# A gated linear-attention stage placed between projections, and per-pair norm and rotation behind the next projection, in a two-block transformer kernel on one Trainium2 core

## The chip, the core and the metric

The kernel runs on one core of one Trainium2 chip. The core has a matrix engine (TensorE, PE in the profile, with its weight loads as PEld), a vector engine (VectorE, DVE), a scalar engine (ScalarE, ACT), GpSimd (POOL), and SyncE (SP), which here issues the weight transfers. The time is the device time of one execution in microseconds (us). Each engine works through its own instruction list in order; semaphores tie the lists together.

## What is computed

Two blocks of two layers each over 256 tokens of width 1024, all in 32-bit floats. Four mixers (differential attention, sparse attention, "even" and "odd") alternate with four expert stages. The change touches the even and the odd mixer, so only these are shown, cut.

```python
def even_mixer(x, w_in, ...):
    h = x @ w_in
    c_q, c_kv, k_pe, gq, gk, gv, g_lr, gr = _split(h, EVEN_SPLITS)   # 256,128,32,256,256,512,32,512
    q  = (rms_norm(c_q, mla_q_norm) @ w_uq)      # 8 heads, 64 plain + 32 rotated
    kv = (rms_norm(c_kv, mla_kv_norm) @ w_ukv)   # 8 heads, keys 64, values 64
    o_mla = mla_attention(...)                   # softmax attention over 256 tokens
    la_f = log_sigmoid(lr_f @ gate_w_fwd + gate_b_fwd) / 16     # la_b likewise
    o_f = gla_chunked(qh, kh, vh, la_f)          # 4 heads, key 64, value 128, 4 chunks of 64
    o_b = flip(gla_chunked(flip(qh), flip(kh), flip(vh), flip(la_b)))
    o_gla = rms_norm(o_f + o_b, gla_norm) * silu(gr)
    return concatenate([o_mla, o_gla])           # then @ w_o, residual, layer norm

def gla_chunked(q, k, v, log_a):
    cum = cumsum(log_a)                          # within a chunk
    qg, kg = q * exp(cum), k * exp(-cum)
    att = where(tri, qg @ kg.T, 0)
    u = (k * exp(last - cum)).T @ v              # the chunk's update of the state
    o = att @ v + qg @ state_before_the_chunk    # state = decay * state + u, chunk by chunk

def odd_mixer(x, w_in, ...):
    q, k, v = _split(x @ w_in, ODD_SPLITS)       # 1024, 256, 256
    q, k = rms_norm per head of 64, then apply_rope
    # grouped attention, 16 query and 4 key heads
```

## The kernel before, in words

The program is one hand-ordered list for each engine; nothing schedules it. Activations lie transposed in SBUF (`xT`, `hT`, `qT`, `kT`, `oT`, `yT`: 128 partitions by 8 pieces by 256 tokens). Weights flow through a ring of 12 slots of 1 MB each (`ring`): SP issues the transfer of slot n as soon as slot n-12 has been used (`slot_used`), in the order in which the jobs were declared. A **job** is one slice of a projection, at most 256 columns of a weight: `project(js)` on PE runs its matmuls into PSUM bank 0 or 1 in turn (16 matmuls of 128 by 128 by 256 for a full slice, L869), and `evacuate(js)` on ACT copies each bank out (L282). PE may start job j when job j-2 is evacuated.

**Even mixer.** PE runs the ten jobs of `w_in` (the slices for the compressed query and key, the shared key, gq, gk, two of gv, the gate's low rank, two of gr), then `partition_norms(1)`, the rms norms of the two compressed vectors, then the jobs of `w_uq` and `w_ukv` with rotations between them, then `attention("mla")`, then `gla_stage()`, then `partition_norms(2)` (rms norm of the gated output times silu), and only then the output projection `even_out`.

`gla_stage` is a chain over three engines: PE computes the gate's logits (L1310, L1312, 8 matmuls), ACT and DVE turn them into log decays (L1692 to L1697, L2167), PE sums them per chunk (L1320), ACT and DVE form qg, kg and kd (L1700 to L1704, L2174 to L2183), PE computes scores (L1331) and four transposes for each direction, DVE masks and copies (L2187, L2189), PE computes updates (L1344), DVE runs the state recurrence (L2200, L2202), PE computes the outputs (L1356 and L1362: 16 matmuls of 128 columns and 24 of 64), and DVE copies them out (L2210).

A norm along partitions (`pns`) takes: squares on ACT (L1556); `pn_sums` on PE (L908), matmuls with the squares as weights and one or two columns of ones; a root on ACT (L1564); a reciprocal on DVE (L1866); `pn_spread` on PE (L922), which spreads the factors over the partitions; and one product per vector on DVE (L1873). A rotation is one matmul on PE (L881) and three DVE instructions (L1857 to L1859).

**Odd mixer.** PE runs four query jobs, two key jobs and one value job, then all sums, then spread and rotation for six pairs of head pieces one after another; the attention begins when DVE has finished the last rotation (L2378, L1012).

The two output projections are followed by a layer norm, the router, and an expert stage whose weights (4 groups of 48 slots, `ring<-in_w`) come through the same ring.

Of the kernel before, what the change touches and what calls it, by code (L numbers as in the profile page):

```python
# [16 lines left out]
P = 128  # L17
T = 256
# [110 lines left out]
def program(nc, A, out):  # L129

    ctx = ExitStack()
    with ctx:
# [251 lines left out]
        for _ in ADA_STEP["nsa"]:  # L384
# [20 lines left out]
        job(ew[:, 0:256], 8, 256, mm_T(xT, 8, [(0, P, 0, 0), (P, P, 0, T)]),  # L405
            copy_to((whole, scr[:, 0:512])), need=("h_ready", 5))
        job(ew[:, 256:384], 8, 128, mm_T(xT, 8, [(0, P, 0, 0)]),
            copy_to((lambda b: ps[:, b, 0:T], ckvT[:, 0, :])))
        job(ew[:, 384:416], 8, 32, mm_T(xT, 8, [(0, 32, 64, 0)]),
            copy_to((lambda b: ps[64:96, b, 0:T], kpe[64:96, :])))  # L410
        ev_kpe = len(jobs) - 1
        job(ew[:, 416:672], 8, 256, mm_T(xT, 8, [(0, P, 0, 0), (P, P, 0, T)]), copy_to((whole, scr[:, 1024:1536])))
        job(ew[:, 672:928], 8, 256, mm_T(xT, 8, [(0, P, 0, 0), (P, P, 0, T)]), copy_to((whole, scr[:, 1536:2048])))
        for s in range(2):
            job(ew[:, 928 + 256 * s:1184 + 256 * s], 8, 256, mm_V(xT, 8, 256),
                copy_to((lambda b: ps[:, b, :].rearrange("p (a n) -> p a n", a=TT), gv[:, :, 256 * s:256 * s + 256])))
        job(ew[:, 1440:1472], 8, 32, mm_T(xT, 8, [(0, 16, 0, 0), (16, 16, 0, T)]),
            copy_to((lambda b: ps[0:16, b, :], rt[0:16, 0:512])))
        ev_lr = len(jobs) - 1
        for s in range(2):  # L420
            job(ew[:, 1472 + 256 * s:1728 + 256 * s], 8, 256, mm_T(xT, 8, [(0, P, 0, 0), (P, P, 0, T)]),
                copy_to((whole, hfl[:, 1024 + 512 * s:1536 + 512 * s]), func=ACT.Silu))
# [63 lines left out]
        dense(ow, xT, qT, 4, ("h_ready", 7))  # L486
        for s in range(2):
            job(ow[:, D + 128 * s:D + 128 * s + 128], 8, 128, mm_T(xT, 8, [(0, P, 0, 0)]),
                copy_to(*twice(kT[:, 2 * s:2 * s + 2, :])))
        job(ow[:, D + 256:D + 512], 8, 256, mm_V(xT, 8, 256), copy_to((whole, vt[:, 0:512])))  # L490
        vo = vt[:, 0:512].rearrange("p (a n) -> p a n", a=TT)
        ph["odd_out"] = len(jobs)
# [53 lines left out]
        r_odd = len(ropes)  # L546
        for s in range(6):
            ropes.append((pair_dst(qT if s < 4 else kT, s % 4), 2, 0, P, K("rot64"), K("cos_g"), K("sin_g"),
                          ("pn_done", 8 + s + 1)))
# [5 lines left out]
        for s in range(4):  # L555
# [4 lines left out]
                    ("job", ph["even"])))  # L560
        pns.append(([ckvT[:, 0, :]], K("ones")[:, 0:1], 128, [(ckvT[:, 0, :], col("mla_kv_norm_2"), ckvT[:, 0, :], None)],
                    ("job", ph["even"] + 1)))
# [4 lines left out]
        for s in range(6):  # L567
            o = pair_dst(qT if s < 4 else kT, s % 4)
            pns.append(([o], K("ones64")[:, 0:P:64], 64, [(o, col("gqa_q_norm_2" if s < 4 else "gqa_k_norm_2"), o, None)],
                        ("job", ph["odd"] + s)))  # L570

        pn_batch = [range(0, 4), range(4, 6), range(6, 8), range(8, 14)]

        def pn_columns(i, c, tt):

            batch = next(b for b in pn_batch if i in b)
            at = 0
            for x in range(batch[0], i):
                at += pns[x][0][0].shape[-1] // T * TT * pns[x][1].shape[-1]
# [3 lines left out]
        def pn_width(batch):  # L583
            last = batch[-1]
            return pn_columns(last, pns[last][0][0].shape[-1] // T - 1, TT - 1).stop
# [58 lines left out]
        soft["mla"] = [vt[:, 1024:2048], flat(oT)[:, 1024:2048]]  # L644
# [21 lines left out]
        kdt = [sg[:, 512 * d:512 * d + 512].rearrange("p (a n) -> p a n", a=TT) for d in range(2)]  # L666
# [1752 lines left out]
```

## Time and profile before

| | us |
|---|---|
| median of 3 runs | 2433.51 |
| lowest, highest | 2432.26, 2434.05 |
| the profiled execution's own time | 2425.88 |
| its span in the profile | 2424.1 |
| PE busy | 1852.0 (76%) |
| DVE busy, ACT busy | 429.3, 400.1 |
| mean granted TensorE clock | 0.878 of full speed |

The even mixer up to its output projection lies between 1007.3 and 1181.9 us of the span; the odd mixer's projections, norms and rotations between 1742.9 and 1820.0. In the rows below, PE is the matmul engine; the chain of waits gives a start, a duration and what ran; a count (x) counts instruction records, and a 32-bit matmul leaves two of them. "PEclk" is the share of full TensorE speed granted, 0.50 being 1.2 GHz and 1.00 being 2.4 GHz.

### The profile page before, as it was taken

The page shows a single profiled execution, that of the slowest core. Times are in us where ns is not written, and L with a number is a line of the kernel's source. Part 1 is how long each engine was busy: PE and PEld are TensorE (multiplying, and loading weights), DVE is VectorE, ACT ScalarE, POOL GpSimd, SP SyncE. Part 2 cuts the span into 40 slices and gives each one's busy share as a digit, 9 for nine tenths or more (in the row PEclk, how much of TensorE's full clock was granted, in tenths as well). Part 3 has the DMA queues.
Part 4 walks back from the last instruction along what each step waited for, and adds up shares of the span by engine and source line. Part 5 has one row for each costly group of instructions (what it writes and reads, how often), then busy time and mean ns, then how long its engine had stood idle before and what let it go on. Part 6 is the DMA issues. An engine that isn't in the chain of part 4 may idle for free.

```text
span 2424.1 us, 31041 instructions
## 1 busy us (share of the span) xinstructions
PE 1852.0 (76%) x13139; PEld 1174.3 (48%) x13139; DVE 429.3 (18%) x960; ACT 400.1 (17%) x822; POOL 0.6 (0%) x5
## 2 busy tenths in 40 slices
PE   5988898988989798797975766656688756675555
PEld 4857655567576455575852323212476523232122
DVE  2232211113622010105120101000124201010001
ACT  3032211113521110114030101000113301010001
POOL 0000000000000000000000000000000000000000
PEclk9998899998989999998788888787889888787888
DMA  9675699986527999931149999999931499999993
GB/s 357 209 273 213 280 403 396 393 269 225 192 104 289 422 370 420 322 122 35 52 173 421 412 421 412 421 422 422 326 105 50 158 421 412 421 411 421 422 422 154
DMA packets 184039, 737.94 MB, mean 304 GB/s; under 512 B 27708, under 2 KB 95208, under 8 KB 108904
## 3 DMA queue, kind: packets, MB, share of 16 engines
q1 hardware_dynamic: 183196, 734.31, 77.1%
q8 instruction: 98, 1.61, 0.3%
q10 hardware_dynamic: 716, 1.79, 0.2%
q14 instruction: 29, 0.24, 0.0%
HBM read 826.23 MB, written 1.05 MB: 341 GB/s over the span
## 4 chain that ended last, share of the span: by engine, by line
PE 54%; DMA 32%; DVE 7%; ACT 3%; SPq 2%; issue 2%; ACTq 0%; POOLq 0%; DVEq 0%
DMA ring<-in_w 22%; PE ps L869 18%; DMA ring<-in_moe_w_up 10%; PE ps L1179 6%; PE ps L1268 6%; PE ps L1291 3%; PE ps L852 2%; PE ps L1165 2%; PE ps L970 2%; PE ps L1150 2%; PE ps L1189 2%; PE ps L1206 1%; PE ps L934 1%; SPq L805 1%; PE ps L1106 1%
## 5 line engine op out<-in xcount | busy, mean ns | idle before, releaser
L1268 PE MATMUL ps<-ring,ptb 128*32 128x512 f32 x2048 | 303.3, 749 | 224.2 <-DMA ring<-in_w 216.8
L1268 PEld LDWEIGHTS ps<-ring,ptb 128*32 128x32 f32 x2048 | 86.1, 133 | 435.9 <-issue 433.6
L1291 PE MATMUL ps<-ring,kT 128*32 128x512 f32 x1024 | 156.2, 769 | 81.8 <-DMA ring<-in_w 81.7
L869 PE MATMUL ps<-xT,ring 128*128 128x256 f32 (+2 forms) x640 | 145.1, 389 | 17.1 <-DVE yT L2143 9.5
L869 PEld LDWEIGHTS ps<-xT,ring 128*128 128x128 f32 (+2 forms) x640 | 119.8, 189 | 42.3 <-DVE yT L2143 11.1
L1291 PEld LDWEIGHTS ps<-ring,kT 128*32 128x32 f32 x1024 | 40.8, 137 | 190.1 <-issue 189.0
L1179 PE MATMUL ps<-ring,yT 128*32 128x256 f32 x1536 | 97.0, 411 | 34.6 <-DMA ring<-in_moe_w_up 27.6
L869 PE MATMUL ps<-oT,ring 128*128 128x256 f32 x512 | 114.7, 384 | 3.8 <-DVE oT L1873 1.6
L869 PE MATMUL ps<-hT,ring 128*128 128x256 f32 x480 | 108.4, 384 | 5.3 <-ACT hT L1534 5.3
L1179 PE MATMUL ps<-ring,vt 128*32 128x256 f32 x1536 | 92.9, 400 | 21.8 <-DMA ring<-in_moe_w_up 19.7
L869 PEld LDWEIGHTS ps<-oT,ring 128*128 128x128 f32 x512 | 98.3, 193 | 18.3 <-DVE oT L1876 1.9
L869 PEld LDWEIGHTS ps<-hT,ring 128*128 128x128 f32 x480 | 91.4, 192 | 24.3 <-issue 11.1
L2137 DVE TENSOR_TENSOR kT<-pb,ps 128x1024 f32<-128x1024 f32 x8 | 9.8, 1222 | 517.8 <-ACT pb L1683 517.8
L1165 PE MATMUL ps<-Dp,oT 128*128 128x256 f32 x384 | 92.6, 398 | 6.2 <-DVE Dp L2069 6.2
L1179 PEld LDWEIGHTS ps<-ring,yT 128*32 128x32 f32 x1536 | 57.8, 118 | 77.3 <-issue 54.9
L1683 ACT ACTIVATE pb<-ps 128x1024 f32<-128x1024 f32 x8 | 8.2, 1024 | 507.7 <-PE ps L1268 507.7
L1189 PE MATMUL ps<-pn,qT 128*128 128x256 f32 x384 | 89.2, 385 | 1.8 <-ACT qT L1670 1.8
L1206 PE MATMUL ps<-ring,kT 128*32 128x512 f32 x768 | 87.4, 595 | 2.1 <-DVE kT L2090 2.1
L1179 PEld LDWEIGHTS ps<-ring,vt 128*32 128x32 f32 x1536 | 54.9, 115 | 62.4 <-issue 37.3
L1165 PEld LDWEIGHTS ps<-Dp,oT 128*128 128x128 f32 x384 | 75.8, 202 | 17.0 <-issue 6.4
L1189 PEld LDWEIGHTS ps<-pn,qT 128*128 128x128 f32 x384 | 71.0, 190 | 21.3 <-issue 12.6
L2143 DVE TENSOR_TENSOR yT<-yT,ps 128x2048 f32<-128x2048 f32 x8 | 18.3, 2288 | 317.9 <-PE ps L1300 317.9
(396 smaller groups left out, 1951.6 us busy)
## 6 DMA issues: line engine op xcount, KB each, us to landing
ring<-in_w SPq DMA_DIRECT2D x384, 1024.0 KB
ring<-in_moe_w_gate SPq DMA_DIRECT2D x96, 1024.0 KB
ring<-in_moe_w_up SPq DMA_DIRECT2D x96, 1024.0 KB
ring<-in_moe_w_down SPq DMA_DIRECT2D x96, 1024.0 KB
ring<-in_ada_w SPq DMA_DIRECT2D x48, 1024.0 KB
ring<-in_diff_w_in SPq DMA_DIRECT2D x12, 1024.0 KB
ring<-in_w_o SPq DMA_DIRECT2D x8, 1024.0 KB
ring<-in_ple_gate_w SPq DMA_DIRECT2D x8, 1024.0 KB
```

The costliest lines, as they stand in the source:

```text
L805: sp.dma_start(ring[:, (n0 + s) % RING, :], w[l, 4 * i + (4 * groups[0] + j)][:, SLOT * kk:SLOT * kk + SLOT])\
L852: return nc.tensor.transpose(dst, src, ident[0:k, 0:k])
L869: last = mmul(o, l, r, start=start, stop=stop)
L934: last = mmul(ps[:, 2, 0:T], K("ones"), sq[:, T * c:T * c + T], start=(c == 0), stop=(c == C - 1))
L970: last = mmul(dst[32 * j:32 * j + 32, :], cpad[:, k, :], ada_view(n)[:, k % 2, T * j:T * j + T], start=(k == 0), stop=(k == C - 1))
L1150: last = mmul(ps[:, 4 + k // 4, P * (k % 4):P * (k % 4) + P], h_tokk[:, tt, k, :], Dg[:, tt, :], start=(tt == 0), stop=(tt == 1))
L1165: last = mmul(ps[:, bank + k % 4 // 2, T * (k % 2):T * (k % 2) + T], h_tokk[:, tt, k, :], Dp[:, tt, :], start=(tt == 0), stop=(tt == 1))
L1179: last = mmul(ps[32 * j:32 * j + 32, a, 0:ff], xs[:, k, s0 + 32 * j:s0 + 32 * j + 32], w[j][:, ff * k:ff * k + ff], start=(k == 0), stop=( ...
L1189: last = mmul(ps[:, 2 + c // 2, T * (c % 2):T * (c % 2) + T], Yg[:, P * c:P * c + P], Cgb[:, g % 2, :], start=(g == 0 and c % 2 == 0), sto ...
L1206: last = mmul(ps[32 * j:32 * j + 32, 6 + h, :], hidT[:, c, 32 * j:32 * j + 32], w[j][:, D * c + 512 * h:D * c + 512 * h + 512], start=(c = ...
L1268: last = mmul(ps[32 * j:32 * j + 32, 2 * a + h, 0:width], xg[:, k, 32 * j:32 * j + 32], w[j][:, ff * k2 + width * h:ff * k2 + width * h + ...
L1291: last = mmul(ps[32 * j:32 * j + 32, 6 + h, :], hidT[:, c, 32 * j:32 * j + 32], w[j][:, D * c2 + 512 * h:D * c2 + 512 * h + 512], start=(c ...
```

## The change

It reorders the jobs and the stages and does the same arithmetic.

- The job of the gate's low rank is declared and run first, then gq, gk, gv, the compressed query and key, the shared key and gr. `gla_stage` on PE is cut into five pieces (gates, sums, scores, updates, outputs), each after one or two projection jobs. ACT's part is cut likewise; DVE's part is called before its norms and before the attention.
- Norms 4 to 7 (compressed vectors and gated outputs) become one batch behind the job gr[0]; their spreads come behind gr[1]. The squares of the first two go to a part of `vt`.
- Scores and outputs of the gated stage go through the heads in pairs (h even and odd alternate). The updates of the second direction go to PSUM banks 2 and 3.
- In the odd mixer the two key jobs come first; each pair has its own batch: its sums, then the next projection job, then the rotation of the pair before and its own spread. The value job is run as two halves of 128 columns, so that there are six projection pieces behind the sums.
- The MLA attention's second probability buffer moves from `oT` to the first half of `hT`.

```diff
-        job(ew[:, 0:256], 8, 256, mm_T(...), copy_to((whole, scr[:, 0:512])), need=("h_ready", 5))
-        ... (ckv, kpe, gq, gk, gv x2, lr, gr x2 in this order)
+        ev_lr = job(ew[:, 1440:1472], 8, 32, mm_T(xT, 8, [(0, 16, 0, 0), (16, 16, 0, T)]),
+                    copy_to((lambda b: ps[0:16, b, :], rt[0:16, 0:512])), need=("h_ready", 5))
+        ev_gq = job(ew[:, 416:672], ...)
+        ... (gk, gv x2, cq, ckv, kpe, gr x2 in this order)
...
-        dense(ow, xT, qT, 4, ("h_ready", 7))
         for s in range(2):
-            ... copy_to(*twice(kT[:, 2 * s:2 * s + 2, :])))
-        job(ow[:, D + 256:D + 512], 8, 256, mm_V(xT, 8, 256), copy_to((whole, vt[:, 0:512])))
+            ... copy_to(*twice(kT[:, 2 * s:2 * s + 2, :])), need=("h_ready", 7) if s == 0 else None)
+        dense(ow, xT, qT, 4, None)
+        for s in range(2):
+            job(ow[:, D + 256:D + 512], 8, 256, mm_V(xT, 8, 256, 128 * s, 128), ..., new=(s == 0), last=(s == 1))
...
-        pn_batch = [range(0, 4), range(4, 6), range(6, 8), range(8, 14)]
+        pn_batch = [range(0, 4), range(4, 8)] + [range(i, i + 1) for i in range(8, 14)]
...
# PE, scores of the gated stage
-                    for h in range(4):
-                        for tt in range(TT):
+                    for c, tt in itertools.product(range(2), range(TT)):
+                        for h in (2 * c, 2 * c + 1):
...
# PE, even mixer
-            project(range(ph["even"], ev_uq))
-            partition_norms(1)
+            project([ev_lr, ev_gq])
+            gla_gates()
+            project([ev_gk, ev_gv[0]])
+            gla_sums()
+            project([ev_gv[1]])
+            gla_scores()
+            project([ev_cq])
+            gla_updates()
+            project([ev_ckv, ev_kpe])
+            gla_outputs()
+            project([ev_gr[0]])
+            pe.wait_ge(S("gla_evac"), 2)
+            pn_sums(1)
+            project([ev_gr[1]])
+            for i in pn_batch[1]:
+                pn_spread(i)
             project(range(ev_uq, ph["even_out"]))
             ropes_until(r_odd)
             attention("mla")
-            gla_stage()
-            partition_norms(2)
+            pe.wait_ge(S("o_evac"), o_after["mla"])
...
# PE, odd mixer
-            project(span["odd"])
-            pn_sums(3)
+            project(span["odd"][0:2])
             for s in range(6):
+                pn_sums(2 + s)
+                project(span["odd"][s + 2:s + 3])
+                ropes_until(r_odd + s)
                 pn_spread(8 + s)
-                if s:
-                    ropes_until(r_odd + s)
             ropes_until(r_end)
...
# ACT, even mixer
+            evacuate([ev_lr, ev_gq])
+            gla_gates()
+            evacuate([ev_gk, ev_gv[0]])
+            gla_decays()
+            evacuate([ev_gv[1], ev_cq])
+            pn_square(4)
+            evacuate([ev_ckv])
+            pn_square(5)
+            evacuate([ev_kpe, ev_gr[0]])
+            pn_square(6)
+            pn_square(7)
+            pn_roots(1)
+            evacuate([ev_gr[1]])
...
# ACT, odd mixer
+            evacuate(span["odd"][0:1])
+            for s in range(6):
+                pn_square(8 + s)
+                evacuate(span["odd"][s + 1:s + 2])
+                pn_roots(2 + s)
...
# DVE, odd mixer
-            pn_inverse(3)
             for s in range(6):
+                pn_inverse(2 + s)
+                ropes_until(r_odd + s)
                 partition_norm(8 + s)
-                if s:
-                    ropes_until(r_odd + s)
```

How PE's list reads at the two places. First the even mixer, PE before: `xT,ring` and `ring,xT` are projection jobs, `sqb` norm sums, `pn` spreads.

```order
L869 MATMUL ps<-xT,ring 128x256 x24
L869 MATMUL ps<-xT,ring 32x256 x8
L869 MATMUL ps<-xT,ring 128x256 x32
L869 MATMUL ps<-ring,xT 128x256 x32
L869 MATMUL ps<-xT,ring 16x256 x16
L869 MATMUL ps<-xT,ring 128x256 x32
L908 MATMUL ps<-cst,sqb 128x1 x6
L922 MATMUL ps<-cst,pn 128x128 x4
```

The same place of the changed kernel, from the job behind the gates on.

```order
L885 MATMUL ps<-xT,ring 128x256 x16
L885 MATMUL ps<-ring,xT 128x256 x16
L1337 MATMUL ps<-cst,oT 128x128 x8
L885 MATMUL ps<-ring,xT 128x256 x16
L1350 MATMUL ps<-sqb,ptb 128x128 x8
L868 MATMUL ps<-cst,vt 128x128 x4
L1350 MATMUL ps<-sqb,ptb 128x128 x8
L868 MATMUL ps<-cst,yT 128x128 x4
L885 MATMUL ps<-xT,ring 128x256 x16
L1366 MATMUL ps<-hT,pb 64x128 x32
L885 MATMUL ps<-xT,ring 128x256 x8
L885 MATMUL ps<-xT,ring 32x256 x8
```

Sums (L1337), scores and transposes (L1350, L868) and updates (L1366) now each stand behind a projection job of 16 matmuls (two of 8 behind the updates); before they stood together behind the attention.

Second the odd mixer, PE before, from the projections to the last rotations.

```order
L869 MATMUL ps<-xT,ring 128x256 x80
L869 MATMUL ps<-ring,xT 128x256 x16
L908 MATMUL ps<-cst,sqb 128x2 x24
L922 MATMUL ps<-cst,pn 64x128 x16
L881 MATMUL ps<-qT,cst 128x512
L922 MATMUL ps<-cst,pn 64x128 x8
```

And the changed kernel, from the third query job to the attention.

```order
L885 MATMUL ps<-xT,ring 128x256 x16
L897 MATMUL ps<-qT,cst 128x512
L938 MATMUL ps<-cst,pn 64x128 x8
L924 MATMUL ps<-cst,sqb 128x2 x4
L885 MATMUL ps<-ring,xT 128x128 x16
L897 MATMUL ps<-qT,cst 128x512
L938 MATMUL ps<-cst,pn 64x128 x8
L924 MATMUL ps<-cst,sqb 128x2 x4
L885 MATMUL ps<-ring,xT 128x128 x16
L897 MATMUL ps<-qT,cst 128x512
L938 MATMUL ps<-cst,pn 64x128 x8
L897 MATMUL ps<-qT,cst 128x512
```

The 24 sum matmuls in one block became six blocks of four, each ahead of a projection piece; the value job of 16 matmuls with 256 columns became two of 16 with 128.

## Rows read from the trace of the kernel before

**Rows 1.** The page, part 2: DMA engines' busy tenths in 40 slices.

```profile
DMA  9675699986527999931149999999931499999993
```

**Rows 2.** Chain of waits, even mixer: start us, duration us, what ran.

```profile
1007.33 64.72 PE ps L869 x288
...
1077.83 3.73 PE ps L869 x8
...
1101.38 2.01 PE ps L1012 x8
...
1122.58 0.66 PE ps L1310 x2
...
1181.93 16.02 PE ps L869 x64
...
1198.81 6.91 PE ps L869 x32
```

**Rows 3.** Timeline 1122 to 1150: start, busy us, engine, line, operation, [idle before].

```profile
1127.96 0.60 ACT L1692 ACTIVATE pn<-ps 128x512 f32<-128x512 f32 x1 [7.14 <-PE ps L1312]
...
1130.25 1.28 ACT L1697 ACT_TABLE_LOAD   x1
...
1132.08 0.62 ACT L1697 ACTIVATE pb<-pb 128x512 f32<-128x512 f32 x1
...
1135.14 0.60 ACT L1700 ACTIVATE vt<-ps 128x512 f32<-128x512 f32 x1 [1.15 <-PE ps L1320]
...
1141.17 0.68 DVE L2183 TENSOR_TENSOR yT<-yT 128x512 f32<-128x512 f32 x1
...
1149.37 1.25 DVE L2202 SCALAR_TENSOR_TENSOR kT<-kT,misc,ps 128x128 f32<-128x128 f32 x4
```

**Rows 4.** PE groups by shape, 1100 to 1235: records, busy us, mean ns, idle before.

```profile
L1362 PE MATMUL ps<-sqb,kT 64*128 64x64 f32 x48 | 11.9, 416 | 0.0
L1356 PE MATMUL ps<-qT,hT 128*128 128x128 f32 x32 | 9.3, 441 | 2.2 <-DVE kT L2202 2.2
...
L1331 PE MATMUL ps<-sqb,ptb 64*128 64x128 f32 x32 | 4.5, 447 | 2.4 <-DVE vt L2183 2.4
...
L1344 PE MATMUL ps<-hT,pb 64*64 64x128 f32 x64 | 2.3, 278 | 0.8 <-DVE qT L2189 0.8
```

**Rows 5.** Windows, PE alone: length, busy us (records), PEclk, DMA share, GB/s.

```profile
1148.00:1151.00 3.00, 0.79 (x18) 1.00 0.00 0
...
1154.00:1157.00 3.00, 3.00 (x14) 0.50 0.00 0
...
1790.00:1792.00 2.00, 2.00 (x11) 0.51 0.85 360
```

**Rows 6.** Timeline, PE pieces that price small matmuls.

```profile
1073.32 1.50 PE L908 MATMUL ps<-cst,sqb 128*128 128x1 f32 x12 [1.29 <-ACT sqb L1556]
...
1111.24 1.89 PE L1012 MATMUL ps<-kT,qT 96*128 96x256 f32 x8
...
1804.24 1.09 PE L922 MATMUL ps<-cst,pn 128*64 128x128 f32 x16
...
1835.93 1.13 PE L1012 MATMUL ps<-kT,qT 64*128 64x256 f32 x8
```

**Rows 7.** Chain of waits, odd mixer.

```profile
1742.90 44.74 PE ps L869 x192
...
1788.83 9.34 PE ps L908 x48
...
1812.14 0.76 DVE kT L1873
...
1814.97 0.76 DVE kT L1873
...
1820.00 2.10 PE ps L1012 x8
```

**Rows 8.** Timeline, last layer's gather: 16 matmuls of 128 columns.

```profile
1911.36 4.49 PE L1150 MATMUL ps<-Dp,oT 128*128 128x128 f32 x32
```

More of the change, by code:

```diff
@@ L1 @@
+import itertools
 import math
@@ L412, in program @@
[L412 to L422, printed above, removed]
+        ev_lr = job(ew[:, 1440:1472], 8, 32, mm_T(xT, 8, [(0, 16, 0, 0), (16, 16, 0, T)]),
+                    copy_to((lambda b: ps[0:16, b, :], rt[0:16, 0:512])), need=("h_ready", 5))
+        ev_gq = job(ew[:, 416:672], 8, 256, mm_T(xT, 8, [(0, P, 0, 0), (P, P, 0, T)]),
+                    copy_to((whole, scr[:, 1024:1536])))
@@ new lines, in program @@
+        ev_gk = job(ew[:, 672:928], 8, 256, mm_T(xT, 8, [(0, P, 0, 0), (P, P, 0, T)]),
+                    copy_to((whole, scr[:, 1536:2048])))
+        ev_gv = [job(ew[:, 928 + 256 * s:1184 + 256 * s], 8, 256, mm_V(xT, 8, 256),
+                     copy_to((lambda b: ps[:, b, :].rearrange("p (a n) -> p a n", a=TT),
+                              gv[:, :, 256 * s:256 * s + 256]))) for s in range(2)]
+        ev_cq = job(ew[:, 0:256], 8, 256, mm_T(xT, 8, [(0, P, 0, 0), (P, P, 0, T)]),
+                    copy_to((whole, scr[:, 0:512])))
@@ new lines, in program @@
+        ev_ckv = job(ew[:, 256:384], 8, 128, mm_T(xT, 8, [(0, P, 0, 0)]),
+                     copy_to((lambda b: ps[:, b, 0:T], ckvT[:, 0, :])))
+        ev_kpe = job(ew[:, 384:416], 8, 32, mm_T(xT, 8, [(0, 32, 64, 0)]),
+                     copy_to((lambda b: ps[64:96, b, 0:T], kpe[64:96, :])))
+        ev_gr = [job(ew[:, 1472 + 256 * s:1728 + 256 * s], 8, 256, mm_T(xT, 8, [(0, P, 0, 0), (P, P, 0, T)]),
+                     copy_to((whole, hfl[:, 1024 + 512 * s:1536 + 512 * s]), func=ACT.Silu)) for s in range(2)]
@@ L485, in program @@
         ow = A["w_in_odd_2"][0]
[L486 removed]
         for s in range(2):
             job(ow[:, D + 128 * s:D + 128 * s + 128], 8, 128, mm_T(xT, 8, [(0, P, 0, 0)]),
[L489 to L490 removed]
+                copy_to(*twice(kT[:, 2 * s:2 * s + 2, :])), need=("h_ready", 7) if s == 0 else None)
+        dense(ow, xT, qT, 4, None)
         vo = vt[:, 0:512].rearrange("p (a n) -> p a n", a=TT)
+        for s in range(2):
+            job(ow[:, D + 256:D + 512], 8, 256, mm_V(xT, 8, 256, 128 * s, 128),
+                copy_to((lambda b: ps[:, b, 0:T].rearrange("p (a n) -> p a n", a=TT), vo[:, :, 128 * s:128 * s + 128])),
+                new=(s == 0), last=(s == 1))
         ph["odd_out"] = len(jobs)
@@ L1546, in norm, with pn_square, pn_roots @@
                 gain(n)
-            def partition_norms(b):
-                for i in pn_batch[b]:
-                    srcs, need = pns[i][0], pns[i][4]
-                    await_need(act, need)
-                    if i >= 2:
-                        act.wait_ge(S("pn_mm"), i - 1)
-                    for a, s in enumerate(srcs):
-                        n = s.shape[-1]
-                        last = func(sqb[:, 512 * (i % 2) + n * a:512 * (i % 2) + n * a + n], s, ACT.Square)
-                    last.then_inc(S("pn_sq"), 1)
+            def pn_square(i):
+                srcs, need = pns[i][0], pns[i][4]
+                await_need(act, need)
+                if i >= 2 and i not in range(4, 8):
+                    act.wait_ge(S("pn_mm"), i - 1)
+                for a, s in enumerate(srcs):
+                    n = s.shape[-1]
+                    last = func(pn_squares(i)[:, n * a:n * a + n], s, ACT.Square)
+                last.then_inc(S("pn_sq"), 1)
+            def pn_roots(b):
                 act.wait_ge(S("pn_mm"), pn_batch[b][-1] + 1)
@@ L1565, in partition_norms @@
                 last.then_inc(S("pn_std"), 1)
+            def partition_norms(b):
+                for i in pn_batch[b]:
+                    pn_square(i)
+                pn_roots(b)
             def attention(name):
```

101 lines of the change are left out of this document (52 added, 49 removed).

## The prediction, made before the changed kernel was run

> **What bounds the kernel now.** I read the page's DMA row first. It is at 9 in the expert stages and falls to 3, 1, 1, 4 and again to 3, 1, 4 (slices 17 to 20 and 29 to 31 of 60.6 us) in the two mixers that the change touches [rows 1]. There the ring is full, so transfers wait for slots and not PE for transfers. The chain of waits then says what bounds these stretches: PE and what it waits for. The even mixer starts its projections at 1007.33 and its output projection at 1181.93, so it takes 174.6 us. Of that the ten jobs take 64.7, the first norm until 1077.8 about 5.8, the query and key jobs until the attention 23.5 (1077.83 to 1101.38), the attention 21.2 (to 1122.58), and the gated stage with its norm 59.3 (1122.58 to 1181.93) [rows 2]. In the last part the engines take turns: ACT works while PE waits, then DVE, then PE [rows 3]. The odd mixer takes 77.1 us from 1742.90 to 1820.00: 44.7 of projections, 9.3 of sums, then a DVE chain in which one pair takes 1814.97 - 1812.14 = 2.83 [rows 7].
>
> A second thing is in these stretches: TensorE's clock. Between 1154 and 1157 PE is busy 3.00 of 3.00 us with the outputs of the gated stage and still runs at 0.50 (1.2 GHz), although it was at 1.00 before they began; the same in the odd mixer's sums [rows 5]. So a pile of small matmuls costs twice over.
>
> **Prices.** A full projection job of 16 matmuls takes 6.91 us at full clock, so a matmul of 256 columns 0.43; two jobs behind a half-clock stretch took 16.02 instead of 13.82, so a fall costs the dense work behind it 2.2 [rows 2]. A matmul of 128 columns takes 4.49 / 16 = 0.28 at full clock [rows 8] and 9.3 / 16 = 0.58 at half; one of 64 columns 11.9 / 24 = 0.50, nearly all at half clock, so 0.25 at full [rows 4]. A sum of one column takes 1.50 / 6 = 0.25 at full clock [rows 6] and 9.34 / 24 = 0.39 mostly at half [rows 7]. Eight paired spreads take 1.09 [rows 6].
>
> **The even mixer after the change, PE's list added up.** Ten jobs: 64.7, unchanged. Gates: 8 x 0.43 = 3.5. Sums: 8 x 0.28 = 2.2. Scores: 16 matmuls of 64 rows, 4.5 before [rows 4], and 8 transposes x 0.28 = 2.2. The heads now alternate between the two row halves; attention scores show what that does, 1.89 for four matmuls of 96 rows and 1.13 for four of 64 rows that alternate [rows 6]. By that ratio of 0.6 scores come to 4.5 x 0.6 = 2.7, and 4.9 with the transposes; without it 6.7. I take 5.4. Updates: 2.3 [rows 4]. Outputs: 21.2 at half clock, 16 x 0.28 + 24 x 0.25 = 10.5 at full, and 8.1 if the 64-column ones also gain the 0.6. Here the trace shows neither end in the new surroundings: before, the stage began at full clock and fell at once [rows 5], but after five microseconds in which PE was mostly waiting; now a dense job stands before it. I take 13, nearer to the full-clock end. Norm: 14 sums x 0.25 = 3.5, 12 spreads x 0.28 = 3.4, one rotation 0.4. Query and key jobs to the attention: 23.5 less 2 x (3.73 - 1.73) = 4.0, since the first two of them ran at half clock (3.73 each for four matmuls that cost 4 x 0.43 = 1.73) [rows 2], so 19.5. Attention: 21.2. One and a half falls of the clock: 3.3. The sum is 64.7 + 3.5 + 2.2 + 5.4 + 2.3 + 13 + 3.5 + 3.4 + 0.4 + 19.5 + 21.2 + 3.3 = 142.4. That is 32.2 less than 174.6. The output projection now follows the attention and not a half-clock stretch, which saves its 2.2: 34.4.
>
> **What hides the other engines' parts, and by how much.** All from the start of the projections. PE ends the gates at about 19.8 and needs the log decays 13.8 later; ACT and DVE took 1127.96 to 1132.70 and 0.7 more, and get one more table load of 1.28 [rows 3]: 6.7, a margin of 7. The decays took 1135.14 to 1141.85, 6.7, with another load of 1.28 ahead [rows 3]; the first direction needs 5.3 of these 8.0 and PE comes 8.0 after its first sums (1.1 + 6.9), so a margin of 2.7, and as much for the second. This is the tightest place: ACT must also copy two jobs out (0.6 each) in between. If it is missed, PE waits at the scores with the query and key jobs queued behind it. The state recurrence (3.4 before 1150.62 [rows 3]) stands beside two jobs of 8 matmuls, 6.9 together. ACT gets three more table loads in the mixer and one before the layer norm's root; all stand where ACT waits for PE. On DVE the two gated products (about 2.9) now stand ahead of the rotations; four rotations of 2.1 each follow in 19.5 of PE work, so they are covered.
>
> **The odd mixer.** Projections 44.7. The value job in halves costs 32 x 0.28 - 6.9 = 2.1 more. Sums 24 x 0.25 = 6.0; five spreads 5.5; four rotations of 512 columns 4 x 0.87 = 3.5. Behind the last half stands what nothing covers: rotation 0.87, DVE rotation and product 2.83, rotation 0.87, DVE rotation 2.83 - 0.76 = 2.07, latencies 0.3, together 7.0. Sum 68.8 against 77.1: 8.3 less. ACT and DVE need 3 to 4 us per pair against 9 of PE. I take off 1.3 for a fall at the value halves: 7.0.
>
> **Queues.** SP issues the same slots in a new order, the small one of 32 columns first in the even mixer and the two key slices first in the odd one. PE waits for no transfer in either stretch before, and each wide slot is now needed later, not sooner. The next expert stage finds its 11 slots loaded, since they are issued as projection slots come free.
>
> **The sum.** 34.4 + 7.0 = 41.4. From the profiled execution's own 2425.9 that gives 2384.5; the median of the runs shown is 7.6 above that execution, so 2433.5 - 41.4 = 2392.
>
> **A rule weighed.** The rows show a busy PE at half clock for the whole of the outputs [rows 5]. The Trainium skill, page "TensorE: Matmul & The Clock Gate", section "What's actually happening", says that the clock follows how busy PE has been, and that activity releases it. By that rule the new mixers, in which PE hardly ever idles, would run at full clock throughout. By that rule the trace does not agree, since there a busy PE stayed slow.
>
> **The rivals.**
> 1. *Full clock throughout.* With a dense job in front of every piece the clock never falls. Outputs 8.1 to 10.5, scores 4.9, no falls: 133.7 to 136.1 in the even mixer, 68.8 in the odd. Taking the lower, 40.9 + 2.2 + 8.3 = 51.4 saved: 2382. For it: the ten jobs in a row take 64.7 where 144 matmuls x 0.432 are 62.2, so a dense stretch pays the fall once. Against it: the half-clock rows [rows 5]. The page named above would have this one.
> 2. *The clock falls in the gated pieces.* Outputs stay at 21.2 (8.2 more), three more jobs pay 2.2 (6.6), and the query jobs start at half clock as before (4.0): 18.8 less saved, 22.6 in all: 2411.
> 3. *A cover is missed.* ACT is late at the scores and again at the norm, 5 us each: 2402.
> 4. *Slower.* Each small piece, 5 in the even and 6 in the odd mixer, pulls the clock down for itself and for the job behind. Even: gates 6.9, sums 4.6, scores 9.1, updates 2.3, outputs 21.2, norm 5.4 + 7.0, rotation 0.9, query jobs 23.5, attention 21.2, jobs 64.7 + 5 x 2.2 = 177.8, with the 2.2 behind the attention a loss of 1. Odd: sums 3.4 more, four jobs 8.8, the value halves at 0.58 instead of 0.28 9.6, spreads 6: 27.8 more than 68.8, a loss of 19.5. Together 20 slower: 2454. It decides from the point where nearly every piece does it. Against it: four matmuls between output jobs leave the next at 6.91 [rows 2].
> 5. *The expert stage takes it back.* If its transfers did not start sooner, the gain would vanish in the wait for weights: about 2430. Against it: the idle DMA in the mixers [rows 1], whose slots come free as PE moves on.
>
> **Chances.** Forecast 0.50; full clock 0.22; clock falls 0.15; cover missed 0.07; slower 0.03; expert stage 0.03. A change within 0.2% (5 us) can't be told from none here. Cases one to three and the forecast are all faster: 0.94, with 0.02 for the same and 0.04 for slower. The range goes from the full-clock case, 2380, to the case of falls, 2412.
>
> **What would show it right or wrong.** The output projection should start about 142 us behind the projections' start, the odd attention about 70. Right: no PE wait over 1 us inside the gated pieces; the outputs between 10 and 16 us; the sums of a pair near 1.0. Wrong: an idle PE in front of the scores (cover), the outputs above 20 us with jobs of over 8 behind (clock), or more waiting for the expert weights than before.

## The result, and the profile of the changed kernel

The changed kernel takes 2376.85 us (median of 4 executions, 2374.32 to 2380.30), the one before 2432.89 beside it (4 executions, 2428.78 to 2434.05). The ratio is 0.978, with a 95% interval from 0.9762 to 0.9797: faster by 2.2%, 56 us by the medians. The forecast was 41.4 us less and 2392; the time lies 3 us below the lower end of its range. The profiled execution took 2377.43, with a span of 2375.7 and a mean granted clock of 0.887 (0.878 before). Against the profiled execution before (2425.88) that is 48.5 us less. The same program timed again later gave 49.9 less (below), so the saving is between 48 and 56 us. The profiled execution before is itself one of the quicker ones; what that does to the account stands below, under the offset.

The page's part 2, first the granted clock and then the DMA engines, tenths in 40 slices:

```profile
PEclk8999799999898999999978888878899879888878
DMA  9766599996544999943269999999922599999993
```

The gaps in the DMA row are shallower than in [rows 1]: 4, 3, 2, 6 where 3, 1, 1, 4 stood, and 2, 2, 5 for 3, 1, 4. The mixers have shrunk around them.

The chain of waits through the even mixer (start us, us, what ran) answers to [rows 2]:

```profile
1010.14 15.86 PE ps L885 x64
...
1028.35 0.80 PE ps L1327 x2
1029.15 0.85 PE ps L1325 x2
...
1030.86 16.13 PE ps L885 x64
1046.99 1.78 PE ps L1337 x16
...
1055.68 1.09 PE ps L1350 x16
1056.78 0.58 PE ps L868 x4
...
1065.95 1.96 PE ps L1366 x64
1067.91 7.22 PE ps L885 x32
1075.13 1.09 PE ps L1379 x8
1076.22 0.81 PE ps L1387 x12
...
1082.74 7.10 PE ps L885 x32
...
1090.39 3.52 PE ps L924 x28
1093.91 10.07 PE ps L885 x32
...
1125.72 5.42 PE ps L1028 x16
...
1146.18 14.08 PE ps L885 x64
```

L885 is a projection job, L1325 and L1327 the gates, L1337 the sums of the decays, L1350 the scores, L1366 the updates, L1379 and L1387 the outputs, L924 the norm's sums, L1028 the attention. A duration is the time to the next piece in the chain, and each piece begins where the one before ends: PE waits nowhere in the gated pieces. The clock is not whole everywhere: the gates go from 0.43 to 0.85 us each halfway through, and two stretches of jobs take 16.13 instead of 13.82 and 10.07 instead of 6.91. Such a stretch at half clock is called a fall below. The mixer takes 1146.18 - 1010.14 = 136.0 us instead of 174.6, and the output projection behind it starts with two jobs in 14.08 instead of 16.02 [rows 2].

The windows over the outputs (length, PE busy and records, PEclk, DMA share, GB/s):

```profile
1070.00:1075.00 5.00, 5.00 (x24) 1.00 0.49 161
1075.00:1083.00 8.00, 8.00 (x83) 1.00 0.48 170
```

Where [rows 5] had 0.50, this has 1.00 throughout. The outputs end after 1082.74 - 1075.13 = 7.6 us. Before, they took 20.2 (1150.67 to 1170.83); the 21.2 of the prediction adds the records of [rows 4], which overlap by a little.

What hides the engines' work beside them, from the timeline (start, busy us, engine, what, [idle before]):

```profile
1037.10 0.68 DVE L2226 SCALAR_TENSOR_TENSOR oT<-ps,pb 128x512 f32<-128x512 f32 x1
...
1051.54 0.68 DVE L2241 TENSOR_TENSOR ptb<-yT,vt 128x512 f32<-128x512 f32 x1
...
1054.22 0.68 DVE L2241 TENSOR_TENSOR ptb<-yT,rt 128x512 f32<-128x512 f32 x1
```

The log decays are there at 1037.8 and PE uses them at 1046.99: 9.2 us to spare, priced at 7. The first direction's keys are there at 1052.2 and used at 1055.68, 3.5 to spare (2.7 priced); the second's at 1054.9 for 1057.36, 2.5. The narrow cover was real, and it held.

The odd mixer, chain of waits, answers to [rows 7]:

```profile
1705.06 10.06 PE ps L885 x32
...
1751.69 0.86 PE ps L897 x2
1752.55 1.02 PE ps L938 x16
1753.58 0.98 PE ps L924 x8
1754.56 3.68 PE ps L885 x32
...
1764.78 0.88 PE ps L897 x2
...
1772.49 2.10 PE ps L1028 x8
```

It takes 67.4 us instead of 77.1. A pair costs PE 0.86 of rotation (L897), 1.02 of spread (L938) and 0.98 of sums (L924), where the pile of 24 sums took 9.34 [rows 7]. A half of the value job takes 3.68. Behind the last half stand the waits that nothing covers, and in them the clock falls once more: the last rotation takes 1.68 instead of 0.86, at a mean granted clock of 0.63 (1768.5 to 1770.3).

Elsewhere: the even mixer starts 2.8 us later than before (1010.14 against 1007.33), the stretch from the output projection to the odd mixer is 2.1 us shorter (1.9 of it the output projection), the rest behind the odd attention 0.9 shorter. 2.8 - 38.6 - 2.1 - 9.7 - 0.9 = -48.5, which closes the account of the two profiled executions. The expert stages' waits, in the groups by line (busy, mean ns | idle before, its releaser):

```profile
L1284 PE MATMUL ps<-ring,ptb 128*32 128x512 f32 x2048 | 310.8, 764 | 217.6 <-DMA ring<-in_w 210.3
...
L1307 PE MATMUL ps<-ring,kT 128*32 128x512 f32 x1024 | 150.1, 740 | 88.6 <-DMA ring<-in_w 88.6
```

Together PE waits 298.9 us there for weights. The same two groups (L1268 and L1291) had 216.8 + 81.7 = 298.5 before: nothing was taken back.

### The profile page after: what moved, and what is told of

Its sections match the earlier page's. It is cut to its first block, busy times and chain, and to the rows that moved or that the text cites. A ratio compares the mean times of both kernels' runs of the same rounds, so it can differ in the third digit from the quotient of the medians.

```text
span 2375.7 us, 31114 instructions
## 1 busy us (share of the span) xinstructions
PE 1827.9 (77%) x13171; PEld 1149.2 (48%) x13171; DVE 429.4 (18%) x964; ACT 403.4 (17%) x829; POOL 0.6 (0%) x5
## 4 chain that ended last, share of the span: by engine, by line
PE 54%; DMA 33%; DVE 6%; ACT 3%; SPq 2%; issue 2%; ACTq 0%; POOLq 0%; DVEq 0%
DMA ring<-in_w 23%; PE ps L885 19%; DMA ring<-in_moe_w_up 10%; PE ps L1195 6%; PE ps L1284 6%; PE ps L1307 3%; PE ps L868 2%; PE ps L1181 2%; PE ps L986 2%; PE ps L1166 2%; PE ps L1205 2%; PE ps L1222 2%; PE ps L950 1%; SPq L821 1%; PE ps L1122 1%
## 5 line engine op out<-in xcount | busy, mean ns | idle before, releaser
L1284 PE MATMUL ps<-ring,ptb 128*32 128x512 f32 x2048 | 310.8, 764 | 217.6 <-DMA ring<-in_w 210.3
L1307 PE MATMUL ps<-ring,kT 128*32 128x512 f32 x1024 | 150.1, 740 | 88.6 <-DMA ring<-in_w 88.6
L885 PE MATMUL ps<-xT,ring 128*128 128x256 f32 (+2 forms) x640 | 151.9, 399 | 17.1 <-DVE yT L2202 9.5
L885 PEld LDWEIGHTS ps<-xT,ring 128*128 128x128 f32 (+2 forms) x640 | 122.2, 193 | 44.3 <-issue 11.6
L885 PE MATMUL ps<-oT,ring 128*128 128x256 f32 x512 | 112.8, 380 | 2.7 <-DVE oT L1932 1.6
L885 PE MATMUL ps<-hT,ring 128*128 128x256 f32 x480 | 108.4, 384 | 5.3 <-ACT hT L1570 5.3
L885 PEld LDWEIGHTS ps<-oT,ring 128*128 128x128 f32 x512 | 97.0, 190 | 16.8 <-DVE oT L1984 2.0
L885 PEld LDWEIGHTS ps<-hT,ring 128*128 128x128 f32 x480 | 91.4, 193 | 24.4 <-issue 11.1
L1222 PE MATMUL ps<-ring,kT 128*32 128x512 f32 x768 | 87.4, 595 | 2.1 <-DVE kT L2149 2.1
```

The costliest lines, as they stand in the source:

```text
L885: last = mmul(o, l, r, start=start, stop=stop)
L1222: last = mmul(ps[32 * j:32 * j + 32, 6 + h, :], hidT[:, c, 32 * j:32 * j + 32], w[j][:, D * c + 512 * h:D * c + 512 * h + 512], start=(c = ...
L1284: last = mmul(ps[32 * j:32 * j + 32, 2 * a + h, 0:width], xg[:, k, 32 * j:32 * j + 32], w[j][:, ff * k2 + width * h:ff * k2 + width * h + ...
L1307: last = mmul(ps[32 * j:32 * j + 32, 6 + h, :], hidT[:, c, 32 * j:32 * j + 32], w[j][:, D * c2 + 512 * h:D * c2 + 512 * h + 512], start=(c ...
```

## The experiments

Each run has executions of the kernel before on the same chip beside it, and its ratio is to those. In the expectations of experiments 1 and 2, theory A is that alternating the row halves makes the outputs and scores cheap, theory B that the clock does, by the dense job in front. From experiment 5 on, the theory is that idle time takes the clock down. A dense job is a run of projection matmuls of 256 columns without a pause.

**1. The changed kernel with the heads one after another again.**

```
-                    for c, tt in itertools.product(range(2), range(TT)):
-                        for h in (2 * c, 2 * c + 1):      # scores
+                    for h in range(4):
+                        for tt in range(TT):
...
-                    for d in range(2):
-                        for h in heads:                   # outputs, 128 columns
+                        for d in range(2):                # one head at a time
```

> The changed kernel with one thing undone: scores and outputs of the gated stage go through the heads one after another, as before. Theory A (alternating the row halves is what made these pieces cheap): the 24 64-column matmuls of the outputs take 0.25 each instead of 0.135, so the outputs take 16 x 0.27 + 24 x 0.25 = 10.3 us or more instead of 7.6, the scores' 16 matmuls 3.5 to 4.5 instead of 2.2; the kernel is 4 to 7 us slower than the changed one. Theory B (the dense job in front, by the clock, made them cheap): outputs stay under 8.5 us and the time within 2 us of the changed kernel. If besides the clock falls inside the outputs, they take 13 to 20 us.

Measured: 2383.46 (2377.07 to 2388.30, 4 executions) beside 2430.12 (7), ratio 0.9816 (0.9793 to 0.9838). The chain of waits at the outputs, and the window over them:

```profile
1069.65 0.64 PE ps L1380 x4
1070.30 0.81 PE ps L1386 x6
```

```profile
1070.00:1081.00 11.00, 11.00 (x79) 1.00 0.31 104
```

Eight such pairs take 1081.25 - 1069.65 = 11.6 us at a clock of 1.00, against 7.6 for the alternating ones. So the alternation is worth 4.0 us at full clock, 3.2 of it in the 64-column matmuls: 0.81 us is three of them here (0.27 each) and six in the changed kernel (0.135). The other 0.8 is in the 128-column ones (0.32 against 0.27), which use all 128 rows; why they gain is not shown. The scores, 64 rows and 128 columns, lose 0.1 per direction only (1.19 against 1.09): 2.4 in both directions, where theory A expected 3.5 to 4.5. The clock needed no alternation to hold, so each theory has a part of it. By the medians this run is 3.4 to 6.6 us slower than the changed kernel (2380.08 in experiment 8, 2376.85 in the first result).

One thing the edit does not separate. The two heads of a pair also write to different PSUM banks, and neighbours no longer add to the same place. That accumulation alone costs this much is unlikely: the value halves of the odd mixer add into one bank too, at 0.23 per matmul of 128 columns. But no run alternates the banks without the row halves.

In the same profile the clock did not fall in the gates or norm sums: the two jobs behind the gates took 14.01 (16.13 in the changed kernel's profile) and the last gate job 7.01 (10.07). That is 5.2 us that an execution has or has not, with the same instructions before it.

**2. The kernel before with the alternation alone.**

```
-                    for h in range(4):
+                    for c, tt in itertools.product(range(2), range(TT)):
...
-                for h in range(4):
+                for c, tt in itertools.product(range(2), range(TT)):
+                    o0, heads = T * c + P * tt, (2 * c, 2 * c + 1)
```

> The kernel before with the heads alternating in scores and outputs and nothing else; the stage stays behind the attention. Before, the outputs took 20.2 us, nearly all at 0.50 of the clock. Theory A: 16 x 0.58 + 24 x 0.27 = 15.8 us at half clock, or about 8 if the denser piece also holds the full clock; the kernel is 4 to 13 us faster than before. Theory B: outputs stay near 20 us, since the clock is what sets them, and the kernel is the same within 2 us.

Measured: 2420.56 (2415.12 to 2421.65) beside 2430.12, ratio 0.9954 (0.9938 to 0.9971): 9.6 us. The chain of waits at the outputs and the window:

```profile
1151.47 1.48 PE ps L1364 x12
1152.94 2.00 PE ps L1356 x8
```

```profile
1150.00:1163.00 13.00, 13.00 (x80) 0.52 0.00 1
```

The outputs take 1163.4 - 1149.9 = 13.5 us, nearly all at half clock, instead of 20.2. The expectation had 15.8 or about 8. A 64-column matmul costs 0.25 (half of [rows 4]), a 128-column one 0.50. The alternation works at either clock, and does nothing for the clock: thirteen microseconds of unbroken PE work stay at 0.52.

That is no general rule for small matmuls. In the kernel before, the scores and transposes a few microseconds earlier also ran without a pause at half clock, and there the clock came back:

```profile
1142.00:1145.00 3.00, 3.00 (x21) 0.51 0.00 0
1145.00:1148.00 3.00, 2.17 (x60) 1.00 0.03 5
```

What tells the two piles apart is not shown.

**3. The even mixer changed alone.** The changed kernel with the odd mixer's order, slices and norms as before.

```
-            project(span["odd"][0:2])
+            project(span["odd"])
+            pn_sums(2)
             for s in range(6):
-                pn_sums(2 + s)
-                project(span["odd"][s + 2:s + 3])
-                ropes_until(r_odd + s)
                 pn_spread(8 + s)
```

> The changed kernel with the odd mixer as before (queries first, all sums after all projections, value job whole). Theory: the two parts add up. The odd mixer goes back from 67.4 to about 77 us, so this is 9 to 11 us slower than the changed kernel, and the even mixer stays at 136. Rival: the expert stages behind the mixers give part back or add to it, so the parts do not add and the difference is under 5 or over 14 us.

Measured: 2388.49 (2386.68 to 2391.30) beside 2430.12, ratio 0.9827 (0.9811 to 0.9844). Its odd mixer takes 76.9 us and its even mixer 136.1, so by the profiles the odd part is worth 9.5. The run lies 11.6 us above the changed kernel's median and 8.4 above the later one of experiment 8: the two parts add up, within that spread.

**4. The value job whole.**

```
-        for s in range(2):
-            job(ow[:, D + 256:D + 512], 8, 256, mm_V(xT, 8, 256, 128 * s, 128),
...
+        job(ow[:, D + 256:D + 512], 8, 256, mm_V(xT, 8, 256), copy_to((whole, vt[:, 0:512])))
```

> The changed kernel with the value job of the odd mixer whole (16 matmuls of 256 columns behind the fifth pair's sums) and nothing between the last pair's sums and its spread. The halves cost 7.36 us together against 7.0 whole, so 0.4 comes back; the last pair's square, root and reciprocal lie open instead: 0.3 + 0.3 + 0.3 and what PE waits for them, some 1 to 2.5 us, partly beside the rotation of the pair before. Theory: 0.5 to 2 us slower than the changed kernel. Rival (the halves cost more than they cover): 0 to 2 us faster.

Measured: 2381.24 (2378.86 to 2385.92) beside 2430.12, ratio 0.9797 (0.978 to 0.9813). The chain of waits at the mixer's end:

```profile
1770.47 1.81 PE ps L894 x2
...
1775.15 1.14 PE ps L894 x2
...
1778.58 2.10 PE ps L1025 x8
```

The odd mixer takes 68.45 us against 67.4. The whole job takes 7.01 here where the halves took 7.36, which is 0.35 of PE, and behind it one more DVE rotation stands uncovered before the attention. The halves are right by 1 us, a size that only the trace shows; the medians can't.

**5. The kernel before with PE kept busy.** 12, 5 and 6 matmuls of 256 columns that nobody reads stand behind the gates, the sums and the updates, where PE waited for ACT and DVE.

```
+            def fill(n, b=0):
+                for x in range(n):
+                    mmul(ps[:, b, 0:T], K("mean"), xT[:, x % C, :], start=True, stop=True)
...
+                fill(12)
...
+                fill(5)
...
+                fill(6, 2)
```

> The kernel before with PE's idle times in the gated stage filled: 12 matmuls of 256 columns behind the gates, 5 behind the sums, 6 behind the updates, whose results nobody reads. Theory (idle time, not the small matmuls, takes the clock down, and small matmuls do not bring it back): the outputs run at 1.00 in their old place too, 11.6 us in the old order of heads as in the run before, against 20.2; with scores, sums, spreads and the first output job the stage shortens by 10 to 14 us and the kernel is as much faster than before. Rival (the small matmuls themselves cannot hold the clock there, whatever precedes): outputs 18 us or more, the kernel within 3 us of before or slower by the filling's length.

Measured: 2420.21 (2416.90 to 2424.89, 10 executions) beside 2429.97 (15), ratio 0.9962 (0.9951 to 0.9974): 9.8 us less, by added work alone. The chain of waits and the window:

```profile
1132.85 8.43 PE ps L1306 x24
...
1153.75 2.79 PE ps L1306 x12
...
1156.98 0.81 PE ps L1369 x6
1157.79 0.64 PE ps L1363 x4
...
1178.54 14.08 PE ps L869 x64
```

```profile
1156.00:1168.00 12.00, 11.94 (x83) 1.00 0.01 1
```

The outputs, untouched and in their old order, take 11.4 us at full clock, as in experiment 1, and the output projection behind starts with 14.08. The gated stage takes 51.4 instead of 59.3, which is 7.9 less, and the output projection gives 1.9 more. The theory had expected 10 to 14 for the stage; its 11.6 for the outputs came true, the rival's 18 did not. So the same small matmuls hold the full clock when PE has been kept busy in front of them and lose it when PE has been waiting. That small matmuls never lose it by themselves is not shown: the gates fall in this profile too. The first filler shows the way up: it starts at half clock, and its twelve matmuls take 8.43 us instead of 5.2.

**6. The gates' bias as one more row of the weights.** The single-row matmuls of the gates (L1327) go; a row of ones stands under the low-rank inputs, and the bias under the weights.

```
-                        mmul(ps[:, 4 + d, T * tt:T * tt + T], lrT[:, d, P * tt:P * tt + P], gw[:, d, :],
-                             start=True, stop=False)
-                        last = mmul(ps[:, 4 + d, T * tt:T * tt + T], K("ones", 1), rows1[0:1, GB0 + T * d:GB0 + T * d + T],
-                                    start=False, stop=True)
+                        last = mmul(ps[:, 4 + d, T * tt:T * tt + T], lr1[:, d, P * tt:P * tt + P], gw[:, d, :],
+                                    start=True, stop=True)
```

> The changed kernel with the gate's bias as a 33rd row of its weights, so that the gates are 4 matmuls of 256 columns instead of 8, four of which had one row. Theory (a piece as long as the eight sometimes lets the clock fall: gates 4.87 instead of 3.5, next job 9.3 instead of 7.0): gates 1.75 us, next job 7.0 in the profile, 1.7 us saved surely and up to 5 in executions with the fall. Rival (the fall came from the first jobs' late start and is met anyway): gates 1.75 to 2.5 with a next job of 9: 1.7 or nothing.

Measured: 2373.16 (2367.97 to 2376.00, 5 executions) beside 2429.97 (15), ratio 0.9762 (0.9745 to 0.9778), against 2380.08 of the changed kernel on the same chip (experiment 8): 6.9 us faster, and the fastest of both kernels and their variants together with the next. The chain of waits:

```profile
1028.19 1.92 PE ps L1327 x8
1030.12 14.01 PE ps L887 x64
...
1090.74 8.70 PE ps L887 x32
```

The gates take 1.9 us instead of 4.9 (3.7 where no fall came, experiment 1), and the two jobs behind them are at full clock. Experiment 7 has the same gates and no fall either (1.92, then 14.01). Two profiles without it, against four of six with it for the eight matmuls, point to the edit and do not prove it; the gain by the medians, 6.9, is more than the 1.8 of work removed. The job behind the norm's sums still pays 1.8.

**7. The same with the norm's sums in two parts.** Six sums ahead of the outputs and eight behind the next job, where all fourteen stood in one run. The outputs go to PSUM banks 4 and 5 instead of 6 and 7.

```
+            pn_sums(1, (4, 5))
             gla_outputs()
             project([ev_gr[0]])
             pe.wait_ge(S("gla_evac"), 2)
-            pn_sums(1)
+            pn_sums(1, (6, 7))
```

> The run with the bias row, and besides the norm's 14 one-column sums in two pieces: 6 ahead of the outputs, 8 behind the first gr job, with the outputs in PSUM banks 4 and 5. Theory (the 3.5 us of sums in one block let the clock fall in some executions, and the second gr job then takes 10.1 instead of 7.0): that job takes 7.0 and the kernel is 0 to 3 us faster than the one with the bias row alone. Rival (one-column matmuls lower the clock in any place): the outputs behind the six sums run at half clock, 13.9 instead of 7.6, and it is 3 to 8 us slower.

Measured: 2372.98 (2370.97 to 2376.80) beside 2429.97, ratio 0.977 (0.9754 to 0.9787). The same as experiment 6, which is the lower end of what the theory allowed. The chain of waits:

```profile
1069.33 1.43 PE ps L926 x12
...
1086.68 1.92 PE ps L926 x16
1088.60 8.70 PE ps L887 x32
```

Six sums ahead of the outputs did them no harm, so the rival is wrong. Eight sums, after a rotation and 0.75 us of waiting, left the same 8.70 behind them, where the theory had 7.0. So shortening the run of sums did not remove this fall. What does is not shown.

**8. The changed kernel once more, in five rounds.** No edit. The question was how much of the 56 us belongs to the change.

> The changed kernel once more, with five rounds beside the kernel before. Theory A (the profiled execution of the kernel before was a lucky one, its median is what counts): the saving is 51 to 56 us, the median of before lies 4 to 7 us above its profiled 2425.9, that of the changed kernel near its profiled 2377.4. Theory B (the changed kernel saves what the two profiled executions show): 46 to 50 us.

Measured: 2380.08 (2377.41 to 2382.83, 5 executions) beside 2429.97 (2422.13 to 2433.28, 15), ratio 0.9796 (0.9781 to 0.9812): 49.9 us, at the upper edge of one expectation and just short of the other. All nine executions of the changed kernel have a median of 2377.9, the 26 of the kernel before beside experiments 1 to 8 and the first result one of 2430.3: 52 us. In this profile too the clock fell in the gates and at the norm's sums.

**9. The wait put back.** The changed kernel with two jobs moved from behind the updates to ahead of them. The outputs then follow the updates at once and wait for the state recurrence on DVE. Nothing else differs, and PE does the same work.

```
-            project([ev_cq])
+            project([ev_cq, ev_ckv, ev_kpe])
             gla_updates()
-            project([ev_ckv, ev_kpe])
             gla_outputs()
```

> The changed kernel with the two jobs of 8 matmuls moved from behind the updates to ahead of them, so that PE waits for the state recurrence in front of the outputs, some 3.4 us, as it did before the change. Theory (idle time takes the clock down and small matmuls do not bring it back): the outputs start at 1.00 and fall after the wait, 10 to 14 us instead of 7.6, and the gr job behind them pays 2 to 3: 3.4 + 3 to 6 + 2 to 3, so 8 to 12 us slower than the changed kernel. Rival (a single wait of 3.4 us leaves the clock alone): outputs 7.6, only the wait is lost, 3 to 4 us slower.

Measured: 2387.74 (2380.94 to 2392.84, 4 executions) beside 2427.90 (7), ratio 0.9824 (0.9801 to 0.9847). The timeline of PE in the profiled execution (2392.84) and the chain of waits behind:

```profile
1080.13 1.16 PE L1379 MATMUL ps<-qT,hT 128*128 128x128 f32 x8 [2.68 <-DVE kT L2261]
1081.22 1.49 PE L1387 MATMUL ps<-sqb,kT 64*128 64x64 f32 x12
1082.64 2.07 PE L1379 MATMUL ps<-qT,hT 128*128 128x128 f32 x8
```

```profile
1084.71 1.48 PE ps L1387 x12
...
1093.15 9.71 PE ps L885 x32
```

After a wait of 2.68 us the outputs begin at full clock (1.16 for the first four) and then fall: 2.07 for the next four, 13.0 us in all, and the job behind takes 9.71 instead of 7.10. These alone are 5.4 + 2.6 + 2.7 = 10.7 us. Against the changed kernel the medians differ by 7.7 to 10.9 us, and the savings beside the kernel before by 9.7 to 15.9. So a short wait ahead of small matmuls can bring the fall back, and the profile prices it. Two of the four executions (2380.94, 2383.54) come near the changed kernel's times, so the fall does not seem to follow such a wait every time; only the slowest was profiled. Its 2392.84 is not all due to the edit: 5.8 us of the 15.4 above the changed kernel's profile stand ahead of the even mixer, which starts at 1015.98 instead of 1010.14, and the mixer itself is 7.7 longer.

## Why the prediction was wrong, by its own steps

**The frame was right.** The gated pieces between jobs, the covers, the full ring and the untouched expert stage came as described. The even mixer was to take 142 us and took 136.0, the odd one 70 and took 67.4, the output projection was to save 2.2 and saved 1.9. No PE wait stands in the gated pieces. What failed is a price.

**The step that failed is the outputs' term: "I take 13".** Measured is 7.6, under the lowest bound (8.1). Of the 6.4 us that the even mixer lies under its sum, this is 5.4. Two things were wrong in it. First the clock: the sentence placed the value between its two ends, for want of a row with a dense job ahead of such a pile; measured is the full clock throughout (1.00). Yet [rows 5] and [rows 3] already had the condition, PE mostly waiting before the fall, and the sentence names it. Experiments 5 and 9 show from both sides that this is what decides: the old kernel with the waits filled holds 1.00 through its outputs, and the new kernel with one wait put back loses it in its profile. Second the alternation: it was a 0.6 for the 64-column matmuls, from attention scores of unequal row counts. It is 0.5 at either clock for the matmuls of the outputs (experiments 1 and 2), and 0.9 for the scores. The four corners, measured, for outputs of 128 and 64 columns, us per matmul:

| | one head after another | alternating | outputs in all |
|---|---|---|---|
| half clock | 0.58 and 0.50 (before) | 0.50 and 0.25 (experiment 2) | 20.2, and 13.5 |
| full clock | 0.32 and 0.27 (experiment 1) | 0.27 and 0.135 (changed) | 11.6, and 7.6 |

Read beside them, the price "nearly all at half clock, so 0.25 at full" was near the 0.27 of the old order, and the alternation comes on top; the forecast's 13 is by chance near the value of a corner that the kernel doesn't have. The table shows another thing: at full clock and in the old order a matmul of 64 columns costs 0.27, and a norm sum of one column costs 0.25 (3.52 for 14). These prices hardly follow the columns.

**The other terms of the even mixer.** Scores with transposes 3.4 (5.4): the 4.5 of [rows 4] was itself mostly at half clock, so that halving by the clock was missing there. Experiment 1 shows that alternation is only 0.2 of it, where the prediction had counted on a ratio of 0.6. Query and key jobs 18.2 (19.5), attention 20.5 (21.2), sums 1.8 (2.2), updates 2.0 (2.3). Norm sums 3.5 and spreads 3.5, as priced. On the other side the falls of the clock: they cost 5.5 (3.3) in jobs and 1.4 in the gates, 4.9 instead of 3.5. They do exist. The rival "full clock throughout" is right for the outputs, wrong in having no falls, and its price of 51.4 and its 2382 are the nearest of all cases. The range's lower end of 2380 is 2 us below that case by the prediction's own numbers. The Trainium skill, page "TensorE: Matmul & The Clock Gate", section "What's actually happening", says that activity releases the clock, and had been weighed against [rows 5], with the verdict that a busy PE stayed slow. Read with what stands ahead of them, most rows agree with it: PE mostly waited before the fall in experiment 9 and in the kernel before, and with a dense job in front the changed kernel's outputs ran at 1.00. Two readings do not agree: small matmuls without a gap left the clock down for 13 us (0.52, experiment 2), and the clock falls in the gates in most profiles of the changed kernel while PE is never idle.

**The odd mixer** gave 9.7 instead of 7.0. A value half costs 0.23 per matmul (3.68 / 16) and not 0.28, which is 1.6, and the other jobs 0.3 more than priced; no fall came at the halves, 1.3; the spreads and sums 0.7 less. The uncovered tail took 7.7, not 7.0: its last rotation ran at the lower clock (1.68 instead of 0.87).

**The offset.** The sum gave 41.4 against the profiled execution, and was set against the median of three. By the profiled executions the miss is 7.1 us (6.4 + 2.7 - 0.3 in the mixers, and -1.7 from elsewhere). By the medians it is 15. The rest lies in the baseline: the kernel before was at 2425.88 in its profile, while its timed executions run from 2422.1 to 2434.1 on all chips. The profiles show where such a spread can come from. The stretch ahead of the even mixer is the same in every run, but for a small set-up in experiments 6 and 7. Yet the mixer starts anywhere from 1007.24 (experiment 8) to 1015.98 (experiment 9), and the profiled execution before has it at 1007.33, nearly the earliest of eleven. To this come falls that one execution has and the next has not (5 us in experiment 1 against the changed kernel). Which stretch made the 7 us was not resolved, since only one execution before was profiled.

**The rivals.** Clock falls in the gated pieces (2411): wrong for the outputs behind a dense job, true for the gates; a wait put back brought the outputs' fall back in the one execution profiled. Cover missed: no, with 2.5 us to spare. Slower: no. The expert stage: 298.9 us of waits against 298.5, no. The halves of the value job were worth 1 us, not a loss.

## What to carry to other kernels

Look at what PE does just before a pile of small matmuls. Directly behind a dense job whose length covered the other engines' turn, the sums, scores, updates and outputs here ran at full clock and hid the others' work too; a wait of 2.68 us in front cost 10.7 in one profile, the wait included. It is no guarantee: in most profiles the clock fell in the gates, and again at the norm's sums, with dense jobs ahead of both. Order matmuls of 64 rows so that neighbours use different halves; that halved those of 64 columns at either clock, and took 8% off those of 128. When pricing a move, take each small matmul's price with the clock of the row that it came from, and scale all terms by it alike, not only the one in focus; and allow for falls that come and go when one profiled execution stands for a median.

## What the hardware showed that was not expected

- Work that PE never pauses in did not bring the clock back: 13.0 us at 0.52 in experiment 2. Yet 12 matmuls of 256 columns did, at 8.43 us instead of 5.2 (experiment 5), and so did scores and transposes in the kernel before (0.51, then 1.00). The outputs in the old order, with a busy PE in front of them, kept 1.00 for 11.4 us (experiment 5) and 11.6 us (experiment 1).
- In eight gate matmuls of 1 and 16 rows, between dense jobs without a pause, the clock fell in the middle of their run (0.43 each, then 0.85), in four of the six profiles that have them in this place (not in those of experiments 1 and 9). In four matmuls of 33 rows it did not, in the two profiles that have them (experiments 6 and 7).
- Adding 23 matmuls of no use made a kernel 9.8 us faster.
- A matmul of 64 rows and 64 columns costs 0.135 us when its neighbour uses the other row half (and another PSUM bank) and 0.27 when it does not.
